# Decay rows of the second mixer: one pass over 64 stacked partitions in place of exact fp32 selection

## The chip, the cores and the metric

The kernel runs on one core of one Trainium2 chip. The time is device time in microseconds of one execution; lower is better. Engines are named as the profile names them: PE is TensorE, PEld its weight load, DVE is VectorE, ACT is ScalarE, POOL is GpSimd, SP is SyncE.

## The reference, cut to what matters

Two transformer-like blocks run one after the other on 512 tokens of width 1024. The change lies in the second block's mixer, in its state-space (Mamba-2) scan with 32 heads of width 64 in 4 groups of 8 heads. The kernel scans in chunks of 128 tokens, which computes the same thing as the reference's chunks of 64:

```python
da = (dt * a).reshape(b, L, G, J)
acs = jnp.cumsum(ak, axis=1)                       # per head, within a chunk
seg = acs[:, :, None] - acs[:, None, :]
decay = jnp.exp(jnp.where(causal, seg, -jnp.inf))
y_diag = jnp.einsum("blsg,blsgj,bsgjp->blgjp", cb, decay, xk)
y_off  = jnp.einsum("blgn,bgjpn,blgj->blgjp", ck, state, jnp.exp(acs))
```

Each head needs its row `acs` (512 values, one per token) on all 128 partitions (for `seg`), and each pair of heads needs its two rows on 64 partitions each (for `exp(acs)`).

## The kernel before, in words

Every engine has one hand-written instruction stream; semaphores order them. Where the same semaphore is reused under another name, the table `GOES_ON` says from which count. PE's stream sets the pace of the second mixer (`pe_mix2`): for each group g it runs the 14 projection units of group g+1 (a unit is 24 matmuls of 128x512: eight blocks of the contraction, each as upper by upper, lower by upper and upper by lower half) and weaves the scan of group g between them. For the last group the units are those of `gate_conv` and `conv_out` (`g_conv`, `conv_out` in the code).

A weight unit comes by DMA into one of six slots of `ring`; ACT copies its upper half into fp32r (`act_upper`), then POOL subtracts to get the lower half in place (`pool_lower`, the tensor `lo_ring`), and only then may PE start the unit (semaphore `split`).

For the scan of group g, with j from 0 to 3 for its pairs of heads and n = 4g + j:

- `all_acs(g, j)` on PE spreads the rows of the two heads of pair j to 128 partitions each: a matmul of `row_acs` (32 partitions, plain fp32) by a one-hot column of the identity, broadcast to 128 columns, and then on top of it an fp32r matmul (`ident_r` by `later_r`) that adds 2^60 above the diagonal.
- `off(g, j)` spreads the two rows of the pair to 64 partitions each (two fp32 matmuls into the two halves of one bank) and then multiplies the states (`y_off`, three fp32 matmuls).
- `diag(g, j)` is eight small fp32 matmuls; it waits for `seg` of DVE's `weighted(g, j)`.
- On ACT, `decays(g, j)` takes the exponentials (eight of 128x128 for `seg`, one of 128x512 for `exp_acs`). ACT reaches it after it has copied out the PE unit ahead of it (`z_out`, `raw_out`). After the exponentials comes the next `act_upper`.
- On DVE, `weighted`, `off_out` and `diag_out` consume what PE and ACT made. Between them DVE runs the 31 taps of the depthwise convolution of group g+1 (`taps`, reading PSUM banks 6 and 7), and after the last tap the 24 steps of the short convolution (`ssm_conv`, SBUF to SBUF). The next group's first unit writes into bank 6 and so waits for the last tap; the next group's taps wait for `gate_u`, that is for its units 1 and 3 and ACT's sigmoid.

PE's order in one group is: units 0 to 3; sums and transposes; units 4 to 6 with `new_state` and `turn_x`; `all_acs(g,0)`; unit 7; `off(g,0)`; `all_acs(g,1)`; and then four times a unit (8 to 11), `diag(g,j)`, `off(g,j+1)`, `all_acs(g,j+2)`; then units 12 and 13. A stretch from one of units 8 to 11 to the next is called a step below.

Of the kernel before, what the change touches and what calls it, by code (L numbers as in the profile page):

```python
# [17 lines left out]
P = 128  # L18
# [44 lines left out]
for _name, _n in COLUMNS:  # L63
# [6 lines left out]
    ("causal", 128), ("levels", 6 * 128), ("reset64", T), ("reset128", T),  # L70
    ("rank4", 4), ("rank8", 8), ("half_col", 2), ("slot_values", 16), ("rank_ids", 64),
]
# [8 lines left out]
for _name, _n in SMALLS:  # L81
# [159 lines left out]
    "expert_in": ("y_hi", 8),  # L241
    "sparse_silu": ("gates_hi", 1),
    "y_picked": ("gates_lo", 1),
}
# [16 lines left out]
def two_block_program(nc, x_d, w_d, mod_w_d, c_d, col_d, con_d, sma_d, lora_d, combine_d, h_d, y_d, x_kept_d, out_d):  # L261
    with ExitStack() as ctx:  # L262
# [24 lines left out]
        def halves(name, over, offset, *shape):  # L287


            return nc.alloc_sbuf_tensor_at(name, [P, *shape], F32R, offset=base[over] + 4 * offset)  # L290
# [1506 lines left out]
        later_r = halves("later", "con", CON["strict64"], P)  # L1797
        ident_r = halves("ident_r", "con", CON["eye64"], P)
        G_UNITS = 14
        X_ORDER = (4, 5, 0, 1, 2, 3)  # L1800
# [12 lines left out]
        def pe_mix2(pe, mm, flip, take, project, project_both, norm_add, rotation):  # L1813
# [47 lines left out]
            def all_acs(g, j):  # L1861
                for o in range(2):
                    h, m = SH * g + 2 * j + o, SH * g + 2 * j + o
                    out = take(("acs", m), ("seg_exp", m + 1))
                    mm(out[:, :], row_to_all(h, NE), row_acs[0:NE, :], True, False)
                    mm(out[:, :].rearrange("p (c t) -> p c t", c=TT), ident_r[:, :],
                       later_r[:, :].rearrange("p (a t) -> p a t", a=1).broadcast_to([P, TT, P]), False, True).then_inc(S("acs_done"), 1)

            def off(g, j):
                n = 4 * g + j  # L1870
                out = take(("exp_acs", n), ("exp_acs", n + 1))
                for o in range(2):
                    last = mm(out[64 * o:64 * o + 64, :], row_to_half(2 * n + o, NE), row_acs[0:NE, :])
                last.then_inc(S("pair_acs_done"), 1)
                out = take(("y_off", n), ("y_off", n + 1))
# [42 lines left out]
            for g in range(NG - 1):  # L1918
# [10 lines left out]
                if g == 0:  # L1929
                    pe.wait_ge(*at_count("ssm_cols", 2))  # L1930
                    pe.wait_ge(*at_count("later", 2))
                all_acs(g, 0)
# [78 lines left out]
        def act_mix2(act, steps):  # L2011
# [63 lines left out]
            def decays(g, j):  # L2075
# [13 lines left out]
                if n >= 2:  # L2089
                    act.wait_ge(*at_count("y_sum", n - 1))  # L2090
                act.activation(exp_acs[n % 2], bank[at[("exp_acs", n)]][:, :], ACT.Exp, scale=-1.0).then_inc(S("exp_acs"), 1)

            upper_through(first + 1)
# [10 lines left out]
            steps.wait()  # L2104
            act.activation(row_tmp[0:NE, :], row_tmp[0:NE, :], ACT.Ln, bias=column("one", rows=NE)).then_inc(S("dt_log"), 1)
            after("conv_a", 0, 0)
            act.wait_ge(*at_count("end_arg", 1))
# [114 lines left out]
        def dve_mix2(dve, steps, modulate, mod_bias):  # L2222
# [105 lines left out]
            def merge_conv(n):  # L2328
# [5 lines left out]
            dve.tensor_scalar(later_r[:, :], constant("causal"), -LATER, LATER, ALU.mult, ALU.add).then_inc(S("later"), 1)  # L2334
            dve.tensor_copy(ident_r[:, :], ident).then_inc(S("later"), 1)
            dve.wait_ge(*at_count("a_pos", 1))
            dve.wait_ge(*at_count("dt_log", 1))
# [12 lines left out]
                              ident[0:NE, 0:NE].rearrange("h (a c) -> h a c", c=1).broadcast_to([NE, NE, TT]),  # L2350
                              last_acs.rearrange("h (a c) -> h a c", a=1).broadcast_to([NE, NE, TT]), ALU.mult).then_inc(S("rows"), 1)
            dve.wait_ge(*at_count("end_exp", 1))
            dve.tensor_tensor(row_dtw[0:NE, :], row_tmp[0:NE, :], row_dt[0:NE, :], ALU.mult).then_inc(S("rows"), 1)
            gate_u(0)
            taps(0, 0, 16)
# [1008 lines left out]
```

## Time and profile before

| | |
|---|---|
| median of 3 runs | 1978.67 us (1976.53 to 1979.45) |
| time of the profiled execution | 1979.14 us |
| its span | 1977.5 us |
| granted clock of PE, mean over the span | 0.956 |
| PE busy | 1802.8 us (91%) |
| DVE busy | 972.1 us (49%) |
| ACT busy | 550.4 us (28%) |
| POOL busy | 851.1 us (43%) |

The time of an execution is 1.6 us more than its span. The mixer's scan lies between about 919 and 1358 us of the span; group 0 is scanned from 919, group 1 from 1032, group 2 from 1151, group 3 from 1270. A row of the trace of PE shows matmuls that overlap in its pipeline, so the distance between two starts, not the duration, is what a matmul takes of PE's time. One fp32 matmul of 512 columns shows as two records.

### The profile page before, as it was taken

The numbers are of one execution on the slowest core, as the hardware profiler recorded it, in microseconds if no ns is written. First come the engines' busy times: TensorE is split into PE (matmuls) and PEld (weight loads), VectorE is DVE, ScalarE is ACT, GpSimd is POOL, SyncE is SP. The second block draws the span as 40 slices with busy tenths as digits, with TensorE's granted clock in tenths as the row PEclk, the third lists the DMA queues.
The fourth block names the chain that finished last, engine by engine and source line by source line (L and its number), as shares of the span: only waits on it lengthen the run. The fifth ranks groups of instructions, "written<-read, shape, count | busy, mean of one in ns | idle before, by whom it ended". The sixth has DMA issues, their size and how long they took to land. (4 is left out here: it accounts for less than half of the span.)

```text
span 1977.5 us, 27738 instructions
## 1 busy us (share of the span) xinstructions
PE 1802.8 (91%) x10956; PEld 1283.4 (65%) x10956; DVE 972.1 (49%) x1363; ACT 550.4 (28%) x979; POOL 851.1 (43%) x408
## 2 busy tenths in 40 slices
PE   6999879998688785999999899999998999999997
PEld 4768668875233222677676676667776678888876
DVE  6476788452011112595767958554888331212101
ACT  3341452422222213423343423563100021010000
POOL 0421246240111110354242432423898668787874
PEclk8989899899799987999999999999999999999999
DMA  8821225315899997122121211213467223333331
GB/s 294 324 71 54 64 98 153 130 45 193 301 410 409 408 409 283 60 86 78 54 75 54 75 58 59 65 54 108 145 205 261 75 75 96 96 96 94 98 96 64
DMA packets 81758, 290.43 MB, mean 147 GB/s; under 512 B 11120, under 2 KB 11120, under 8 KB 81008
## 3 DMA queue, kind: packets, MB, share of 16 engines
q1 hardware_dynamic: 74880, 271.54, 39.5%
q10 hardware_dynamic: 2160, 8.91, 1.2%
q0 software_dynamic: 4608, 8.40, 1.1%
q8 instruction: 83, 1.36, 0.3%
q14 instruction: 27, 0.22, 0.0%
HBM read 282.25 MB, written 14.94 MB: 150 GB/s over the span
## 5 line engine op out<-in xcount | busy, mean ns | idle before, releaser
L2638 PE MATMUL bank<-arena 64*64 64x64 f32 (+4 forms) x1968 | 228.2, 377 | 53.1 <-ACT arena L1687 28.0
L2581 POOL TENSOR_TENSOR lo_ring<-ring,hi_ring 128x1024 fp32r<-128x1024 f32 x52 | 150.7, 2902 | 260.0 <-ACT hi_ring L2575 260.0
L2638 PE MATMUL bank<-h_lo,hi_ring 128*128 128x512 f32 x648 | 255.7, 395 | 0.0
L2638 PE MATMUL bank<-mix_h_hi,lo_ring 128*128 128x512 f32 x576 | 228.2, 396 | 0.0
L2638 PEld LDWEIGHTS bank<-arena 128*64 128x64 f32 (+2 forms) x1968 | 112.8, 156 | 157.1 <-issue 149.5
L2611 POOL TENSOR_TENSOR lo_ring<-ring,hi_ring 128x1024 fp32r<-128x1024 f32 x77 | 203.0, 2636 | 6.0
L2609 POOL TENSOR_TENSOR hi_ring<-ring,col 128x1024 fp32r<-128x1024 f32 x77 | 157.3, 2043 | 78.6 <-PE bank L2638 78.2
L2638 PE MATMUL bank<-mix_h_hi,hi_ring 128*128 128x512 f32 x416 | 166.8, 401 | 10.5 <-POOL lo_ring L2581 6.8
L2247 DVE SCALAR_TENSOR_TENSOR arena<-bank,col,arena 128x511 f32<-128x511 f32 (+14 forms) x240 | 156.5, 722 | 0.0
L2638 PEld LDWEIGHTS bank<-h_lo,hi_ring 128*128 128x128 f32 x648 | 122.2, 189 | 27.6
L2638 PE MATMUL bank<-ffn_h_hi,lo_ring 128*128 128x512 f32 x352 | 139.2, 395 | 0.0
L2638 PE MATMUL bank<-arena,con 64*64 64x64 f32 (+8 forms) x428 | 128.9, 476 | 3.6 <-DVE arena L1503 3.1
L2638 PEld LDWEIGHTS bank<-mix_h_hi,lo_ring 128*128 128x128 f32 x576 | 109.3, 190 | 25.1 <-issue 0.5
L1762 POOL DMA_INDIRECT y_dram<-arena,slot_table x16 | 16.1, 1004 | 222.6 <-DVE arena L1725 222.6
L2505 DVE TENSOR_TENSOR arena<-arena,bank 128x512 f32<-128x512 f32 x22 | 15.1, 687 | 189.7 <-PE bank L2638 189.7
L2581 POOL TENSOR_TENSOR lo_ring<-ring,hi_con 128x1024 fp32r<-128x1024 f32 x18 | 51.8, 2880 | 113.0 <-ACT hi_con L2575 113.0
L2638 PEld LDWEIGHTS bank<-mix_h_hi,hi_ring 128*128 128x128 f32 x416 | 78.5, 189 | 32.2 <-POOL lo_ring L2581 7.7
L2638 PE MATMUL bank<-ffn_h_hi,hi_ring 128*128 128x512 f32 x232 | 91.3, 394 | 0.0
L2642 PE MATMUL bank<-con,arena 128*128 128x128 f32 x320 | 52.3, 305 | 35.1 <-DMA arena<-h_dram,slot_table 14.9
L3084 DVE SCALAR_TENSOR_TENSOR arena<-arena,late 128x1024 f32<-128x1024 f32 x46 | 69.8, 1529 | 26.6 <-DMA arena<-mod_weights_dram 26.5
L2581 POOL TENSOR_TENSOR lo_ring<-ring,hi_ring_1a 128x1024 fp32r<-128x1024 f32 x10 | 26.7, 2674 | 126.4 <-ACT hi_ring_1a L2575 126.4
L1260 POOL TENSOR_TENSOR arena<-xT,con 128x256 f32<-128x256 f32 x48 | 52.1, 1108 | 66.4 <-DVE xT L1161 47.0
(435 smaller groups left out, 3777.6 us busy)
## 6 DMA issues: line engine op xcount, KB each, us to landing
ring<-weights_dram SPq DMA_DIRECT2D x248, 512.0 KB, 3.6
arena<-weights_dram SPq DMA_DIRECT2D x150, 512.0 KB, 11.3
arena<-mod_weights_dram SPq DMA_DIRECT2D x54, 512.0 KB, 4.7
late<-mod_weights_dram SPq DMA_DIRECT2D x42, 512.0 KB, 3.7
arena<-y_dram ACTq DMA_DIRECT2D x8, 512.0 KB, 6.8
xT<-x_dram SPq DMA_DIRECT2D x2, 1024.0 KB, 7.6
xT<-x_dram SPq DMA_DIRECT2D x1, 2048.0 KB, 9.8
h_dram<-arena ACTq DMA_DIRECT2D x4, 512.0 KB, 8.5
```

Of the source, the lines that this page charges most:

```text
L1260: pool.tensor_tensor(four(level_t[:, q, :]), four(ab[:, q, 0:256]), constant("levels", l, 64).rearrange("p (a t) -> p a t", a=1).broadcast ...
L1762: pool.indirect_dma_start(out=y_d, out_offset=bass.IndirectOffsetOnAxis(ap=slot_table[:, PAIRS + p:PAIRS + p + 1], axis=0), in_=y_rows[:, ...
L2247: dve.scalar_tensor_tensor(conv_y[:, k, back:T], u[:, 0:T - back], w, conv_y[:, k, back:T], ALU.mult, ALU.add).then_inc(S("conv_y"), 1)
L2505: dve.tensor_tensor(ffn_act[:, n, :], ffn_silu[:, n % 2, :], bank[at[("ffn_up", n)]][:, :], ALU.mult).then_inc(S("ffn_act"), 1)
L2581: pool.tensor_tensor(ring_r[:, u % RING, :], ring[:, u % RING, :], hi_unit(u).bitcast(F32), ALU.subtract).then_inc(S("split"), 1)
L2609: pool.tensor_tensor(hi, w, column("zero").broadcast_to([P, UNIT]), ALU.add).then_inc(S("split_hi"), 1)
L2611: pool.tensor_tensor(ring_r[:, u % RING, :], w, hi.bitcast(F32), ALU.subtract).then_inc(S("split"), 1)
L2638: return pe.matmul(out, lhsT, rhs, start=start, stop=stop, skip_group_check=True)
L2642: return pe.matmul(out, x, ident, start=True, stop=True, is_transpose=True, skip_group_check=True)
L3084: dve.scalar_tensor_tensor(w, w, 1.0, silu_c2 if 48 <= i < MOD_OUT else silu_c, ALU.mult, ALU.mult, accum_out=mod[:, mod_column(i):mod_col ...
```

## The change

`all_acs` and `off` no longer use plain fp32. The row `acs` is split into an upper part in fp32r (partitions 0 to 31 of `acs_r`) and the rest (partitions 32 to 63), and the selector has two ones per column (`head_r`: the identity of 32 stacked twice), so that one fp32r matmul over 64 partitions adds both parts. For a pair of heads the selector is a 64x128 tile `two_heads_r`, two of them in turn; ACT writes each (64x128) from `head_r`, two pairs ahead. So the pair needs one matmul in place of two. `acs_r` overlays the constant `reset128`, `head_r` the constant `rank_ids` (which is moved for that), the selectors overlay `head_ones` and a part of `sma`. DVE gets three instructions, once: `head_r`, and the upper and lower part of `acs_r`. ACT gets 16.

```diff
-    ("rank4", 4), ("rank8", 8), ("half_col", 2), ("slot_values", 16), ("rank_ids", 64),
+    ("rank_ids", 64), ("rank4", 4), ("rank8", 8), ("half_col", 2), ("slot_values", 16),
...
+        acs_r = halves("acs_r", "con", CON["reset128"], T)
+        head_r = halves("head_r", "con", CON["rank_ids"], NE)
+        two_heads_r = [halves("two_heads0", "con", CON["head_ones"], P), halves("two_heads1", "sma", T, P)]
...
                     out = take(("acs", m), ("seg_exp", m + 1))
-                    mm(out[:, :], row_to_all(h, NE), row_acs[0:NE, :], True, False)
+                    mm(out[:, :], head_r[0:2 * NE, h:h + 1].broadcast_to([2 * NE, P]), acs_r[0:2 * NE, :], True, False)
...
                 out = take(("exp_acs", n), ("exp_acs", n + 1))
-                for o in range(2):
-                    last = mm(out[64 * o:64 * o + 64, :], row_to_half(2 * n + o, NE), row_acs[0:NE, :])
-                last.then_inc(S("pair_acs_done"), 1)
+                pe.wait_ge(*at_count("two_heads", n + 1))
+                mm(out[:, :], two_heads_r[n % 2][0:2 * NE, :], acs_r[0:2 * NE, :]).then_inc(S("pair_acs_done"), 1)
...
-                    pe.wait_ge(*at_count("later", 2))
+                    pe.wait_ge(*at_count("later", 5))
...
                 act.activation(exp_acs[n % 2], bank[at[("exp_acs", n)]][:, :], ACT.Exp, scale=-1.0).then_inc(S("exp_acs"), 1)
+                if n + 2 < 4 * NG:
+                    two_heads(n + 2)
+
+            def two_heads(n):
+
+                act.activation(two_heads_r[n % 2][0:2 * NE, :].rearrange("p (o a) -> p o a", o=2),
+                               head_r[0:2 * NE, 2 * n:2 * n + 2].bitcast(F32).rearrange("p (o a) -> p o a", a=1).broadcast_to([2 * NE, 2, 64]),
+                               ACT.Copy).then_inc(S("two_heads"), 1)
...
+            act.wait_ge(*at_count("later", 3))
+            two_heads(0)
+            two_heads(1)
             after("conv_a", 0, 0)
...
+            dve.tensor_tensor(head_r[0:2 * NE, :], ident[0:2 * NE, 0:NE], ident[0:2 * NE, NE:2 * NE], ALU.add).then_inc(S("later"), 1)
...
+            dve.tensor_copy(acs_r[0:NE, :], row_acs[0:NE, :]).then_inc(S("later"), 1)
             dve.wait_ge(*at_count("end_exp", 1))
             dve.tensor_tensor(row_dtw[0:NE, :], row_tmp[0:NE, :], row_dt[0:NE, :], ALU.mult).then_inc(S("rows"), 1)
+            dve.wait_ge(*at_count("later", 4))
+            dve.tensor_tensor(acs_r[NE:2 * NE, :], row_acs[0:NE, :], acs_r[0:NE, :].bitcast(F32), ALU.subtract).then_inc(S("later"), 1)
             gate_u(0)
```

On PE, between unit 7 and unit 8 of a group, these rows stand before the change (`arena,con` is `row_acs` by the one-hot column; the row of three is `y_off`):

```order
L2638 MATMUL bank<-arena,con 64x512 x2
L2638 MATMUL bank<-arena 128x128 x3
L2638 MATMUL bank<-arena,con 128x512
L2638 MATMUL bank<-later,ident_r 128x512
L2638 MATMUL bank<-arena,con 128x512
L2638 MATMUL bank<-later,ident_r 128x512
L2638 MATMUL bank<-mix_h_hi,hi_ring_51 128x512
```

And with the change at the same place (all line numbers below the new lines are 18 higher):

```order
L2656 MATMUL bank<-acs_r,two_heads_84 128x512
L2656 MATMUL bank<-arena 128x128 x3
L2656 MATMUL bank<-acs_r,head_r 128x512
L2656 MATMUL bank<-later,ident_r 128x512
L2656 MATMUL bank<-acs_r,head_r 128x512
L2656 MATMUL bank<-later,ident_r 128x512
L2656 MATMUL bank<-mix_h_hi,hi_ring_51 128x512
```

Nothing changed its place; two half matmuls became one, and each selecting matmul reads `acs_r` in fp32r.

On ACT, in the first `decays` of group 0, these rows stand with the change; the row L2100 is the new selector, and behind it comes the upper half of the next weight unit (L2593):

```order
L2037 ACTIVATE arena<-bank 128x512
L2088 ACT_TABLE_LOAD
L2088 ACTIVATE arena<-bank,arena 128x128 x8
L2094 ACTIVATE rstd<-bank 128x512
L2100 ACTIVATE two_heads_84<-head_r 64x128
L2593 ACTIVATE hi_ring_51<-ring 128x1024
```

Before, L2575 (the same `act_upper`) followed directly on L2091 (the exponential of `exp_acs`); everything else on ACT kept its order.

## Rows read from the trace of the kernel before

**Rows 1.** The page, part 1: engine, busy us, share, instructions.

```profile
PE 1802.8 (91%) x10956; PEld 1283.4 (65%) x10956; DVE 972.1 (49%) x1363; ACT 550.4 (28%) x979; POOL 851.1 (43%) x408
```

**Rows 2.** Waits of PE in the scan, 900 to 1360 us: us, times, longest.

```profile
PE bank L2638 <- POOL lo_ring L2581: 10.4, 2, 5.7
...
PE bank L2638 <- DVE arena L2247: 1.4, 1, 1.4
```

**Rows 3.** Timeline of PE, three unit starts: start us, us, work, [idle, releaser].

```profile
1120.52 0.47 PE L2638 MATMUL bank<-mix_h_hi,hi_ring 128*128 128x512 f32 x1 [1.40 <-DVE arena L2247]
...
1137.57 0.79 PE L2638 MATMUL bank<-mix_h_hi,hi_con 128*128 128x512 f32 x1 [5.72 <-POOL lo_ring L2581]
...
1259.38 0.79 PE L2638 MATMUL bank<-mix_h_hi,hi_ring 128*128 128x512 f32 x1
```

**Rows 4.** Timeline of POOL, and one row of ACT's.

```profile
1079.70 2.69 POOL L2581 TENSOR_TENSOR lo_ring<-ring,hi_ring 128x1024 fp32r<-128x1024 f32 x1 [5.37 <-ACT hi_ring L2575]
...
1127.56 9.96 POOL L2581 TENSOR_TENSOR lo_ring<-ring,hi_con 128x1024 fp32r<-128x1024 f32 x1 [9.92 <-ACT hi_con L2575]
...
1248.65 12.30 POOL L2581 TENSOR_TENSOR lo_ring<-ring,hi_ring 128x1024 fp32r<-128x1024 f32 x2 [6.44 <-ACT hi_ring L2575]
...
1067.06 2.17 ACT L2085 ACTIVATE arena<-bank,arena 128x128 f32<-128x128 f32 x8
```

**Rows 5.** Timeline of DVE, from group 1's first weighted on.

```profile
1068.30 0.69 DVE L2302 TENSOR_TENSOR arena<-arena 128x512 f32<-128x512 f32 x1 [6.87 <-ACT arena L2085]
...
1077.26 0.69 DVE L2302 TENSOR_TENSOR arena<-arena 128x512 f32<-128x512 f32 x1 [1.69 <-ACT arena L2085]
1078.22 0.69 DVE L2302 TENSOR_TENSOR arena<-arena 128x512 f32<-128x512 f32 x1 [0.27 <-ACT arena L2085]
...
1080.20 2.74 DVE L2320 TENSOR_TENSOR arena<-arena,late 128x512 f32<-128x512 f32 x1
...
1100.10 0.69 DVE L2302 TENSOR_TENSOR arena<-arena 128x512 f32<-128x512 f32 x1 [1.43 <-ACT arena L2085]
...
1114.62 6.38 DVE L2247 SCALAR_TENSOR_TENSOR arena<-bank,col,arena 128x486 f32<-128x486 f32 x10
...
1131.25 4.05 DVE L2263 SCALAR_TENSOR_TENSOR arena<-arena,col 128x512 f32<-128x512 f32 x6
```

**Rows 6.** Waits of DVE in the scan, 900 to 1360 us.

```profile
DVE arena L2302 <- ACT arena L2085: 43.2, 24, 9.6
```

**Rows 7.** Groups by form, PE, 936 to 1345 us: records, busy us, mean ns.

```profile
L2638 PE MATMUL bank<-arena,con 32*128 32x512 f32 x64 | 35.8, 639 | 0.0
...
L2638 PE MATMUL bank<-arena,con 32*64 32x512 f32 x64 | 17.2, 612 | 0.0
```

**Rows 8.** Timeline of PE, group 1, unit 7 to unit 8: start us, us.

```profile
1065.04 1.07 PE L2638 MATMUL bank<-arena,con 32*64 32x512 f32 x4
1066.04 0.94 PE L2638 MATMUL bank<-late,arena 128*128 128x128 f32 x6
1066.91 1.12 PE L2638 MATMUL bank<-arena,con 32*128 32x512 f32 x2
1067.96 0.50 PE L2638 MATMUL bank<-later,ident_r 128*128 128x512 f32 x1
1068.39 1.12 PE L2638 MATMUL bank<-arena,con 32*128 32x512 f32 x2
1069.44 0.50 PE L2638 MATMUL bank<-later,ident_r 128*128 128x512 f32 x1
1069.78 0.40 PE L2638 MATMUL bank<-mix_h_hi,hi_ring 128*128 128x512 f32 x1
1070.02 0.39 PE L2638 MATMUL bank<-mix_h_hi,lo_ring 128*128 128x512 f32 x1
```

**Rows 9.** Stages: us, busy of engines, granted clock.

```profile
1137.50:1142.00 4.50, 4.43 (x13) 3.60 (x14) 0.69 (x1) 1.41 (x2) 4.50 (x3) 0.66 0.00 0
1142.00:1146.00 4.00, 4.00 (x19) 3.20 (x19) 0.00 (x0) 1.06 (x1) 0.21 (x1) 1.00 0.01 1
```

More of the change, by code:

```diff
@@ L242 @@
     "sparse_silu": ("gates_hi", 1),
+    "two_heads": ("totals", 1),
     "y_picked": ("gates_lo", 1),
```

## The prediction

> **What bounds the kernel now.** The page's busy times come first: PE is busy for 1802.8 us of 1977.5, every other engine (PE's own weight load aside) for less than half [rows 1]. So time taken from PE should be time won, unless PE is waiting where the change works. The waits of PE in the scan are few, 10.4 us for POOL's `lo_ring` in two waits and 1.4 us for DVE's taps (L2247) in one [rows 2], but the timeline shows where they stand, and that matters more than their sum. Behind group 1 PE waits 1.40 us at 1120.52, before unit 0 of the next group, for the last taps, and 5.72 us at 1137.57, before unit 2, for POOL [rows 3]. The other wait for POOL, of 4.7 us, is the same one behind group 0.
>
> Why is POOL late? Its subtraction of one weight tile takes 2.69 us at 1079.70, but 9.96 us at 1127.56 and 12.30 us for two at 1248.65 [rows 4]. In both stretches DVE runs its convolution from SBUF to SBUF without a pause, until 1131.25 + 4.05 = 1135.3 in the first [rows 5], and POOL ends at 1127.56 + 9.96 = 1137.5, 2.2 us after DVE stopped. The two exclude each other. It holds the other way too: DVE's L2320 takes 2.74 us at 1080.20 while POOL subtracts from 1079.70 to 1082.4, against 0.69 for another product of the same shape (L2302) [rows 4, 5]. That names the mechanism: the next group's unit 2 is released by DVE's last convolution step, with POOL between them. The Trainium skill says the same (GPSIMD Engine Reference, Specifications): GpSimd's SBUF interfaces are shared with VectorE, and the contention is with DVE instructions that have two SBUF inputs or run in a two-port mode; by that rule the taps, which read PSUM, leave POOL alone, and the trace agrees.
>
> So from `gate_u` of one group to unit 2 of the next the pace is DVE's: taps, the scan's products, taps, convolution, POOL's 2.2 us. PE has a margin of 5.72 us there, DVE has only its waits. Those are on `weighted` (L2302), which waits for ACT, which waits for PE's unit to end: 43.2 us in 24 waits over the four groups [rows 6]. In group 1 they are 6.87 us at 1068.30, 1.69 at 1077.26, 0.27 at 1078.22 and 1.43 at 1100.10 [rows 5].
>
> **The change on PE.** It removes 64 records of 32\*128 (two per matmul, so 32 matmuls) and 64 of 32\*64 [rows 7], and puts in 32 + 16 matmuls in fp32r. The sequence of one `all_acs` runs from 1066.91 to 1069.78, 2.87 us: exact 1.05, masking 0.43, exact 1.05, masking 0.34 [rows 8]. The trace has no fp32r matmul over 64 partitions. Nearest are the projections, 1069.78 to 1070.02, 0.23 to 0.24 us with weight load hidden [rows 8], and the masking matmul, 0.34 behind an exact one and before an fp32r one, 0.43 between two exact ones. From below 4 x 0.23 = 0.92, from above 4 x 0.43 = 1.72. I take 0.34 + 3 x 0.23 = 1.03, since only the first follows an fp32 matmul: 1.84 us won, 16 times. `off` pays 1.00 us for its selection (1065.04 to 1066.04); one fp32r matmul costs 0.43 behind `diag` (three of four) and, because the unit before it hands over faster, about 0.22 behind unit 7: 3 x 0.57 + 0.78 = 2.5 us per group. Together 4 x 1.84 + 2.5 = 9.9 us per group, 39.5 us over four. If instead the new matmul cost nothing less than an exact one, PE would win only the second half of `off` or nothing; that is the other end.
>
> A rule of the Trainium skill prices the same in another way (FP8 and Floating Point Precision, TensorE Precision Notes): a true fp32 matmul makes four passes through the array, one of reduced precision takes one. By it 48 matmuls save three passes each, an estimate of 48 x 3 x 0.23 = 33 us; the rows give more, since 1.05 us is over four times 0.23.
>
> **What of it arrives.** In groups 0 to 2 the next units wait for DVE's chain, so only what DVE waits less counts. `weighted(g,0)` is released by unit 7, which comes 1.84 us earlier (one `all_acs`): the wait falls from 6.87 to 5.0. Each of the following steps is shorter on PE by 1.84 + 0.78 or 0.57, 2.4 to 2.6 us, more than the waits of 1.69 and 1.43 there, which vanish, and with them three gaps of 0.27 between the two heads, as ACT is then ahead. Sum: 1.84 + 1.69 + 1.43 + 3 x 0.27 = 5.8 us per group. From then on DVE has no idle time between the first `weighted` and the end of its convolution, and the remaining 4 us of PE's gain turn into longer waits at `diag`, at unit 0 of the next group (1.40 us in group 1, then some 4) and before unit 2.
>
> Group 0: 5.8. Group 1: 5.8. In group 2 the fp32 sums of the layer norm stand ahead of the unit in question (`g_conv` 2, at 1259.38 [rows 3]); the two subtractions at 1248.65 take 12.30 us, the second of them undisturbed and so about 2.69, and the first, which this unit needs, is done at 1248.65 + 12.30 - 2.69 = 1258.3 [rows 4]. PE was later than POOL by 1.1. With the change POOL is ready at 1252.5 and PE at 1259.4 - 9.9 = 1249.5: 6.9 us won, and a new wait of 3.0. Group 3 has no taps beside it and its convolution is over; there PE sets the pace and all 9.9 arrive. The sum is 5.8 + 5.8 + 6.9 + 9.9 = 28.4 us.
>
> **What is added elsewhere.** ACT gets 16 copies of 64x128. Eight exponentials of 128x128 take 2.17 us, 0.27 each [rows 4], so a copy costs about 0.3. It stands behind `exp_acs`, where ACT then waits for PE's unit anyway; what it delays is `act_upper`, and POOL's subtraction by 0.3, whose tile PE needs only two units later. DVE's three instructions come once, before `gate_u(0)`; no larger than the 128x512 ones of 0.69 [rows 5], and `gate_u` behind them waits for ACT's sigmoid. I cost both at nothing; without that cover they would be 0.3 on each of nine steps, 2.7 us, and at most 3 x 0.69 = 2.1 once.
>
> **Collisions.** POOL's subtraction now starts earlier within a step while DVE runs a little later relative to it, so it no longer meets `diag_out` but may meet `weighted`. Each meeting costs 2.74 - 0.69 = 2.05 us [rows 5]. Three of them per group are in the trace already. I keep three; one less or one more in each of three groups is 6 us either way. The clock: after the wait of 5.72 us PE is granted 0.66 of full speed over the next 4.5 us, so it ran at 1.2 GHz for a part, and then 1.00 [rows 9]; that costs (1 - 0.66) x 4.5 = 1.5 us, and the new wait of 3.0 us in group 2 may bring one more such dip.
>
> Against the profiled execution: 1979.14 - 28.4 = 1950.7. The median of the runs shown is 0.5 us below that execution, less than the runs differ among themselves. I say 1951.
>
> **The rivals.**
> (a) *Forecast*: DVE's chain holds back three groups; 1951, own range 1946 to 1957. Chance 0.55.
> (b) *PE's whole gain arrives*: if the waits for POOL and the taps shrink as much as PE's work, 39.5 us are won: 1939.6. For it speaks PE's 91% busy; against it that PE already waits at 1120.52 and 1137.57, where earlier arrival only lengthens the wait. Partly true if collisions vanish. Chance 0.10, with values from 1939 to 1946.
> (c) *New collisions and dips eat a third*: one more meeting in each of three groups (6 us), a dip in group 2 and another (3 us), loads not hidden in group 3 (4 x 0.7 = 3 us): 28 - 12 = 16 won, 1963; values from 1957 to 1970. For it: a saturated DVE has no idle time left to absorb a meeting. Chance 0.28.
> (d) *No change*: the fp32r matmul over 64 partitions with a broadcast selector costs what it replaces, 32 x 1.05 + 16 x 1.00 = 49.6 us over 48 matmuls, or 1.03 each. Against it: the masking matmul has a broadcast operand too and costs 0.43 at most [rows 8]. 1979; chance 0.03.
> (e) *Slower*: it costs more than those 1.03 us, because the stationary operand, 64 partitions read with a stride of zero, loads slowly in fp32r and nothing hides it. From 1.03 on every further tenth costs 48 x 0.1 = 4.8 us, all of it on PE, which then sets the pace everywhere; at 1.2 us the time is 1979 + 8 = 1987. For it: no row shows such a load. Against it: the one-hot column of before is read the same way, and its load is inside the 1.05. Chance 0.04.
>
> **How the numbers follow.** A difference of 0.2% (4 us) is about what a measurement of this kernel can tell from none. Range: (a) whole, the upper part of (b), the lower half of (c): 1943 to 1961, about 0.79 of the chance. Faster: 0.55 + 0.10 + 0.28 = 0.93; within: 0.03; slower: 0.04.
>
> **What the profile of the changed kernel would show.** Right: the 32 selecting matmuls at 0.23 to 0.43 us from start to start and a step on PE 2.4 us shorter where PE does not wait; no wait of DVE for ACT at L2302 other than the first of a group (near 5 us); in groups 0 to 2 waits of PE at unit 0 of the next group for taps and before unit 2 for POOL, larger in sum than the 10.4 + 1.4 us of now; group 3 shorter by 9.9. Wrong: waits on PE in groups 0 to 2 no longer than now (then (b)); more than three products of DVE over 2 us per group, or a granted clock under 1 in new places (then (c)); a selecting matmul near 1 us (then (d)). The forecast fails above all if DVE's chain is not as full as I read it.

## The result and the profile after

The changed kernel takes 1963.86 us in the median of 6 runs (1960.05 to 1965.68), the kernel before 1980.6 in 6 (1976.53 to 1987.8): a ratio of 0.9923, 95% interval 0.9903 to 0.9942, so about 15 us faster where 28 were forecast. The profiled execution took 1965.68 us with a span of 1964.0, 13.5 less than before.

The page of the changed kernel, part 1, as [rows 1]:

```profile
PE 1783.6 (91%) x10876; PEld 1287.4 (66%) x10876; DVE 990.5 (50%) x1366; ACT 553.5 (28%) x995; POOL 845.9 (43%) x408
```

PE is busy 19.2 us less, not 39.5. Between unit 7 and unit 8 a new wait now breaks the sequence of [rows 8]; one step later, between unit 8 and unit 9 of group 1, it runs through, behind `diag` in place of a unit (start us, us):

```profile
1067.83 0.49 PE L2656 MATMUL bank<-acs_r,two_heads 64*128 64x512 f32 x1
1068.25 0.94 PE L2656 MATMUL bank<-late,arena 128*128 128x128 f32 x6
1069.11 0.49 PE L2656 MATMUL bank<-acs_r,head_r 64*128 64x512 f32 x1
1069.53 0.50 PE L2656 MATMUL bank<-later,ident_r 128*128 128x512 f32 x1
1069.96 0.50 PE L2656 MATMUL bank<-acs_r,head_r 64*128 64x512 f32 x1
1070.39 0.50 PE L2656 MATMUL bank<-later,ident_r 128*128 128x512 f32 x1
1070.73 0.39 PE L2656 MATMUL bank<-mix_h_hi,hi_ring 128*128 128x512 f32 x1
```

From 1069.11 to 1070.73 `all_acs` takes 1.62 us; before it was 2.87, and 1.03 was forecast. Each selecting matmul takes 0.42 or 0.43, and so does the masking one between them. The start of `off` takes 0.42 instead of 1.00, as forecast; behind unit 7 it is 0.42 too (1056.73 to 1057.15), where 0.22 was forecast.

The timeline of PE at its waits around group 1, as [rows 3]:

```profile
1010.09 0.80 PE L2656 MATMUL bank<-mix_h_hi,hi_ring 128*128 128x512 f32 x1 [5.69 <-POOL lo_ring L2599]
...
1059.94 0.49 PE L2656 MATMUL bank<-acs_r,head_r 64*128 64x512 f32 x1 [1.01 <-ACT arena L2088]
...
1111.73 0.76 PE L2656 MATMUL bank<-mix_h_hi,hi_ring 128*128 128x512 f32 x1 [5.46 <-DVE arena L2261]
...
1128.78 0.79 PE L2656 MATMUL bank<-mix_h_hi,hi_con 128*128 128x512 f32 x1 [3.02 <-POOL lo_ring L2599]
```

The wait at 1111.73 was 1.40 us, and the one of 1.01 is new: the second `all_acs` of a group wants a bank that ACT's exponentials have yet to read. It comes at 947.00 and 1179.00 too, with 1.00.

The timeline of DVE in group 1, as [rows 5]; L2316 is `weighted`, L2334 and L2332 are in `diag_out`, L2340 is `group_out`:

```profile
1059.99 0.69 DVE L2316 TENSOR_TENSOR arena<-arena 128x512 f32<-128x512 f32 x1 [5.62 <-ACT arena L2088]
...
1068.64 0.69 DVE L2316 TENSOR_TENSOR arena<-arena 128x512 f32<-128x512 f32 x1 [1.37 <-ACT arena L2088]
...
1071.59 2.77 DVE L2334 TENSOR_TENSOR arena<-arena,late 128x512 f32<-128x512 f32 x1
...
1081.85 1.99 DVE L2332 TENSOR_TENSOR late<-late,rstd 128x384 f32<-128x384 f32 x1
...
1090.74 2.50 DVE L2332 TENSOR_TENSOR late<-late,rstd 128x384 f32<-128x384 f32 x1
...
1094.35 4.88 DVE L2340 SCALAR_TENSOR_TENSOR arena<-arena,col 128x512 f32<-128x512 f32 x4
```

The first wait is 5.62, not 5.0, and the second 1.37, not nothing. An undisturbed L2332 takes 0.56 and four of L2340 2.73 (both in the run with late evacuations below), so these four meetings with POOL cost 2.08 + 1.43 + 1.94 + 2.15 = 7.6 us, and with one more of 0.91 at 1103.72 it is 8.5, where before there were three, 6.2 us.

**An account of PE.** The three stretches below run from `gate_u` of one group to `gate_u` of the next, and the last to the first matmul of `ssm_out`. First the kernel before, then the changed one (stretch, us, PE busy, records, granted clock, DMA share, GB/s):

```profile
918.14:1031.49 113.35, 108.66 (x494) 0.98 0.22 65
1031.49:1150.98 119.49, 112.37 (x507) 0.99 0.20 62
1150.98:1385.69 234.71, 234.06 (x1037) 1.00 0.23 72
```

```profile
914.93:1024.43 109.50, 102.61 (x474) 0.97 0.22 68
1024.43:1143.49 119.06, 109.37 (x487) 0.94 0.21 62
1143.49:1367.64 224.15, 221.63 (x996) 0.99 0.24 75
```

Time minus busy is PE's idle time. One minus the clock, times the stretch, is what the lower clock cost; busy minus that is the work, as at full clock. Over the whole scan, with the clock read in 46 equal slices of each trace (its rounding is then worth a few tenths, where these three rows give 12.7 for the changed kernel's loss):

| kernel | scan | work | clock loss | idle |
|---|---|---|---|---|
| before | 467.6 | 451.6 | 3.5 | 12.5 |
| changed | 452.7 | 421.8 | 11.8 | 19.1 |

So 29.8 us of work are gone, 8.3 came back as clock and 6.6 as idle: 14.9. Outside the scan the changed execution came to it 3.2 us earlier in code that nothing touched, and took 596.4 us behind it where before it was 591.8; the other runs here have 592 to 597 there, so I read nothing into either. A single profile is coarse: ahead of the scan, in code that nothing touched, the clock loss alone lies between 68 and 87 us over the 17 profiles. In slices of 1 us, every stretch of lowered clock in the scans of fourteen of these traces costs 1.7 us or two or three times that; the kernel before pays 1.7 us twice, the changed one seven times. Over whole executions, with the clock and the span of each, seven of the changed kernel (the first run of the next section) lose 100.4 us on average and the 21 of the kernel before beside them 95.9: some 5 us more, rather than 8.3.

### The profile page after: what moved, and what is told of

It is laid out like the page before. It is cut to its first block and busy times, and to the rows that moved or that the text cites. A ratio compares the mean times of both kernels' runs of the same rounds, so it can differ in the third digit from the quotient of the medians.

```text
span 1964.0 us, 27613 instructions
## 1 busy us (share of the span) xinstructions
PE 1783.6 (91%) x10876; PEld 1287.4 (66%) x10876; DVE 990.5 (50%) x1366; ACT 553.5 (28%) x995; POOL 845.9 (43%) x408
## 3 DMA queue, kind: packets, MB, share of 16 engines
q10 hardware_dynamic: 2160, 8.91, 1.2%
## 5 line engine op out<-in xcount | busy, mean ns | idle before, releaser
L2599 POOL TENSOR_TENSOR lo_ring<-ring,hi_ring 128x1024 fp32r<-128x1024 f32 x52 | 145.4, 2799 | 247.3 <-ACT hi_ring L2593 247.3
L2629 POOL TENSOR_TENSOR lo_ring<-ring,hi_ring 128x1024 fp32r<-128x1024 f32 x77 | 203.4, 2641 | 6.0
L2656 PE MATMUL bank<-mix_h_hi,hi_ring 128*128 128x512 f32 x416 | 168.1, 404 | 14.8 <-POOL lo_ring L2599 5.8
L3102 DVE SCALAR_TENSOR_TENSOR arena<-arena,late 128x1024 f32<-128x1024 f32 x46 | 77.7, 1701 | 21.6 <-DMA arena<-mod_weights_dram 21.4
L1726 DVE COPY arena<-bank 128x512 f32<-128x512 f32 x32 | 22.1, 692 | 115.3 <-PE bank L2656 115.3
## 6 DMA issues: line engine op xcount, KB each, us to landing
xT<-x_dram SPq DMA_DIRECT2D x1, 2048.0 KB, 10.3
```

The source lines that it names most:

```text
L1726: dve.tensor_copy(y_rows[:, par, half * 512:half * 512 + 512], bank[4 + half][:, :]).then_inc(S("sparse_y"), 1)
L2599: pool.tensor_tensor(ring_r[:, u % RING, :], ring[:, u % RING, :], hi_unit(u).bitcast(F32), ALU.subtract).then_inc(S("split"), 1)
L2629: pool.tensor_tensor(ring_r[:, u % RING, :], w, hi.bitcast(F32), ALU.subtract).then_inc(S("split"), 1)
L2656: return pe.matmul(out, lhsT, rhs, start=start, stop=stop, skip_group_check=True)
L3102: dve.scalar_tensor_tensor(w, w, 1.0, silu_c2 if 48 <= i < MOD_OUT else silu_c, ALU.mult, ALU.mult, accum_out=mod[:, mod_column(i):mod_col ...
```

## The experiments

The table gives all runs; a ratio is to the kernel before on the same chip beside them (1983.6 us for the first four rows; 1981.2 for dummy matmuls to 19 taps; 1981.65 for off alone and the three combined kernels; 1981.37 for the last three). The four columns at the right are the account, each from its own profiled execution. The four groups of runs come from four chips, so kernels of different groups are best compared by their ratios.

| run | median us | ratio (95%) | scan | work | clock loss | idle |
|---|---|---|---|---|---|---|
| changed, again | 1964.8 | 0.9916 (0.9886 to 0.9947) | 449.6 | 421.7 | 8.5 | 19.4 |
| 128 rows | 1957.33 | 0.9866 (0.9819 to 0.9913) | 444.1 | 407.9 | 10.1 | 26.1 |
| late evacuations | 1971.15 | 0.9931 (0.9911 to 0.9952) | 461.9 | 419.1 | 15.4 | 27.5 |
| all_acs alone | 1968.71 | 0.9928 (0.9905 to 0.9951) | 452.1 | 432.0 | 5.1 | 15.0 |
| dummy matmuls | 1963.17 | 0.9912 (0.9887 to 0.9938) | 449.3 | 431.1 | 6.7 | 11.4 |
| early exponentials | 1955.92 | 0.9885 (0.9857 to 0.9913) | 443.9 | 422.4 | 5.1 | 16.5 |
| before, 19 taps | 1972.88 | 0.9946 (0.9915 to 0.9977) | 462.2 | 451.0 | 5.1 | 6.0 |
| changed, 19 taps | 1954.11 | 0.9854 (0.9815 to 0.9894) | 445.1 | 421.7 | 6.9 | 16.5 |
| off alone | 1984.3 | 1.0016 (0.9992 to 1.0041) | 473.9 | 440.4 | 17.3 | 16.2 |
| 128 rows + early | 1945.26 | 0.9835 (0.9800 to 0.9871) | 431.6 | 406.0 | 6.8 | 18.8 |
| ... + late evacuations in two groups | 1941.83 | 0.9813 (0.9778 to 0.9847) | 430.8 | 404.9 | 8.5 | 17.4 |
| 128 rows + early + dummy matmuls | 1940.07 | 0.9811 (0.9774 to 0.9847) | 428.7 | 414.9 | 3.4 | 10.4 |
| off + early | 1979.6 | 0.9989 (0.9964 to 1.0014) | 465.1 | 440.2 | 10.1 | 14.7 |
| before + early | 1979.9 | 0.9977 (0.9954 to 1.0000) | 467.6 | 450.0 | 5.2 | 12.4 |
| off alone, again | 1986.55 | 1.0018 (0.9994 to 1.0042) | 472.2 | 441.5 | 13.8 | 16.9 |

The column of work is the steadiest: kernels with the same matmuls agree within 3.3 us (419.1 to 422.4 for the changed one and its variants), so smaller differences in it mean nothing.

**The changed kernel again.**

> The changed kernel once more, unaltered, so that the other kernels of this call have it beside them on the same chip. Every theory expects the same time as before within its scatter: 1960 to 1966 us, 0.990 to 0.995 of the kernel before.

1964.8 us, as expected. Its scan is 3.1 us shorter than in the first profile with the same work and idle: the clock alone differed (8.5 against 11.8). That is the grain of a single profile.

**Selectors over 128 partitions.** `acs_r` and `head_r` get zeros in rows 64 to 127, and the two matmuls read all rows:

```diff
-                    mm(out[:, :], head_r[0:2 * NE, h:h + 1].broadcast_to([2 * NE, P]), acs_r[0:2 * NE, :], True, False)
+                    mm(out[:, :], head_r[:, h:h + 1].broadcast_to([P, P]), acs_r[:, :], True, False)
...
-                mm(out[:, :], two_heads_r[n % 2][0:2 * NE, :], acs_r[0:2 * NE, :]).then_inc(S("pair_acs_done"), 1)
+                mm(out[:, :], two_heads_r[n % 2][:, :], acs_r[:, :]).then_inc(S("pair_acs_done"), 1)
```

> The selectors, acs_r and head_r now take all 128 partitions (rows 64 to 127 are zero), nothing else moves. Theory A (a weight load of 64 partitions between matmuls of 128 is not hidden behind the matmul before it): the selecting matmul of two_heads and that of head_r show 0.23 to 0.30 us from the end of the one before to their own, where the changed kernel shows 0.42 to 0.43; a mixer unit's PE work falls by about 0.4 us for all_acs and 0.15 to 0.2 per off start. Rival B (the gap comes from the type or from the stride-zero selector): it stays 0.42. On the time both expect little, as DVE's chain ends the group: A 1958 to 1964 us, B 1960 to 1966.

The timelines tell it best. First PE's and its weight load's rows of the run with 128 rows, in `all_acs` ahead of unit 7:

```profile
1050.60 0.48 PE L2657 MATMUL bank<-acs_r,head_r 128*128 128x512 f32 x1
1050.91 0.40 PE L2657 MATMUL bank<-later,ident_r 128*128 128x512 f32 x1
1051.14 0.40 PE L2657 MATMUL bank<-acs_r,head_r 128*128 128x512 f32 x1
1051.38 0.40 PE L2657 MATMUL bank<-later,ident_r 128*128 128x512 f32 x1
1051.61 0.39 PE L2657 MATMUL bank<-mix_h_hi,hi_con 128*128 128x512 f32 x1
...
1050.91 0.19 PEld L2657 LDWEIGHTS bank<-acs_r,head_r 128*128 128x128 f32 x1
1051.15 0.19 PEld L2657 LDWEIGHTS bank<-later,ident_r 128*128 128x128 f32 x1
```

Then the weight loads of the changed kernel, whose matmuls stand further up:

```profile
1069.53 0.19 PEld L2656 LDWEIGHTS bank<-later,ident_r 128*128 128x128 f32 x1 [0.24 <-issue]
1069.96 0.18 PEld L2656 LDWEIGHTS bank<-acs_r,head_r 64*128 64x128 f32 x1 [0.25 <-issue]
```

With 64 rows each load begins only with its own matmul's row (1069.53, 1069.96) and adds its 0.18 to 0.19 us; with 128 rows it begins one matmul ahead (1050.91 for the matmul of 1051.14) and is hidden, and matmuls follow each other at 0.23 or 0.24, only the first taking 0.31. The type, the broadcast selector and the number of columns are the same in both. The steps at 1050.91 and 1051.38 show 0.23 for the masking matmul too, which the change did not touch: it pays 0.43 between two neighbours of another height, and 0.34 with one behind it only (1070.39 to 1070.73). The pair's selector takes 0.23 behind unit 7 and 0.33 or 0.34 behind the small matmuls of `diag`. Theory A holds and rival B is out; both operands got their 128 rows together, so which of the two counts is not separated. With 1.01 us the whole `all_acs` (1050.60 to 1051.61) now costs what was forecast. The work falls by another 14 us and the time by 7.5, to just below the range of theory A; the rest is idle time again, and the waits for ACT at the second `all_acs` grow from 1.00 to 1.78 us, because PE now comes earlier. DVE's first `weighted` waits 4.82 and 4.85 us here, near the 5.0 of the forecast.

**Evacuations held back.** ACT's `raw_out` of rows 1 to 3, behind which stands `act_upper`, waits for DVE's `off_out` (row 3 in groups 2 and 3 of the units for `group_out`):

```diff
             def raw_out(g, r):
                 i = X_ORDER[r]
+                if g and 0 < r < 4:
+                    act.wait_ge(*(at_count("y_ssm", 4 * (g - 1)) if r == 3 and g > 1 else at_count("y_off", 4 * (g - 1) + r + 1)))
```

> ACT's evacuation in raw_out of rows 1 to 3 is held until DVE has finished its off_out (row 3 in groups 2 and 3: its group_out), so that POOL's subtraction starts later and no longer lies in DVE's weighted and off work. Theory C (meetings of POOL and DVE took the gain back: L2334 2.77 us, L2332 1.99 and 2.50, group_out 4.88 us in group 1 of the changed kernel): DVE's chain from gate_u to the taps' end gets up to 5 us shorter per group, and the time falls by 5 to 15 us, to 1948 to 1958 us. Rival D (meetings only move: POOL's subtraction meets the taps and then holds PE, as PE's 9.96 us wait for POOL in the kernel before): no gain or a loss, 1962 to 1975 us, with longer PE waits for POOL.

Both theories have a part. Rows of this kernel's timelines (DVE in group 1's `diag_out` and `group_out`; then PE, behind group 2):

```profile
1088.87 0.56 DVE L2334 TENSOR_TENSOR late<-late,rstd 128x384 f32<-128x384 f32 x1
...
1090.54 2.73 DVE L2342 SCALAR_TENSOR_TENSOR arena<-arena,col 128x512 f32<-128x512 f32 x4
...
1237.88 0.80 PE L2658 MATMUL bank<-mix_h_hi,hi_ring 128*128 128x512 f32 x1 [11.37 <-POOL lo_ring L2601]
```

In group 1 the meetings are down to 1.3 us from the 8.5 of the changed kernel, but the chain from `gate_u` to the next `gate_u` is 101.6 us against 104.8: of 7.2 us freed, 3.2 arrive and 3.6 became longer waits of DVE (19.2 us against 15.6). But behind group 2 POOL now subtracts inside DVE's convolution, and PE waits 11.37 us with the clock falling behind it. The meetings are real, but taking them away is worth only 1 to 3 us a group; moving POOL's work costs more where it then meets the convolution.

**The two halves apart.** One kernel keeps `head_r` in `all_acs` and puts the two plain fp32 matmuls back into `off`; the other keeps `two_heads` in `off` and puts `row_acs` back into `all_acs`:

```diff
-                mm(out[:, :], two_heads_r[n % 2][0:2 * NE, :], acs_r[0:2 * NE, :]).then_inc(S("pair_acs_done"), 1)
+                for o in range(2):
+                    last = mm(out[64 * o:64 * o + 64, :], row_to_half(2 * n + o, NE), row_acs[0:NE, :])
+                last.then_inc(S("pair_acs_done"), 1)
```

> Only half of the change undone otherwise: head_r for the off starts stays, all_acs goes back to two fp32 matmuls of 64 columns on row_acs per pair of heads, and ACT's copies of two_heads are gone. Theory (the gain comes on DVE's first weighted wait and on PE in proportion to what all_acs saved, 1.25 us of it per unit, off starts the rest): weighted waits 6.85 us again, PE's sum 16 x 1.25 = 20 us longer than in the changed kernel, and the time 1970 to 1976 us. Rival E (ACT's copies cost what they save, or the gain is from off alone): 1960 to 1966 us, like the changed kernel.

My text describes this kernel the wrong way round. What ran has the new `all_acs` and the old `off`, as the diff shows and as its name says; the ACT copies are gone, as written. Its numbers are to be read so: 1968.71 us, of 19.6 us of work saved 15.5 arrive in the scan. On top of it the new `off` brings 3.9 us by the medians (1964.8 with both), but the intervals of the two ratios overlap. In group 1 it even costs: without it `group_out` meets no subtraction, the meetings are 5.8 us and not 8.5, and DVE's chain is 102.4 us and not 104.8.

> The other half of the change: off's start by two_heads stays, with ACT's copies; all_acs takes row_acs in two fp32 selecting matmuls as in the kernel before. By the account of PE from the runs so far (the scan gets shorter by the work saved, less what PE's waits over 0.3 us grow, less half of the time at clock 0.50 that is added), with 16 x 0.57 = 9.1 us saved and waits like the kernel before: 7 to 9 us of the scan, 1970 to 1976 us. Rival (the gain came from the half with all_acs and the ACT copies cost time of their own): no gain, 1978 to 1982 us.

The half in `off` brings nothing: 1984.3 us beside 1981.65, and again:

> Off's start alone once more, unaltered, to see whether its result (1984.3 us) and its clock dips come again: by theory J both do, 1980 to 1986 us with half clock for 20 us or more of the scan; if it was one bad hour of the chip, 1970 to 1976 us.

It repeats, 1986.55 us. Of the work 11.2 and 10.1 us are saved, but 13.8 and 10.3 more than before are lost to the clock and 3.7 and 4.4 to idle. All executions say the same: by their own clocks the ten of each run lose 10.8 and 10.3 us more than the kernel before beside them, and the rest of their time is 7.3 and 6.9 us shorter. The windows of PE in the first of the two runs (stretch, us, PE busy, records, granted clock), around group 1's and group 2's second `all_acs`, where PE waits 0.38 and 0.37 us for ACT:

```profile
1064.00:1068.00 4.00, 3.62 (x13) 0.98 0.46 133
1068.00:1072.00 4.00, 4.00 (x9) 0.50 0.00 0
1072.00:1076.00 4.00, 4.00 (x13) 0.66 0.01 4
...
1192.00:1196.00 4.00, 3.63 (x7) 0.77 0.31 122
1196.00:1200.00 4.00, 4.00 (x10) 0.50 0.00 0
```

So PE ran at 1.2 GHz for a part of it. In the kernel before the same slices around its own place (1060 to 1072) are at 1.00; it has still more of the plain fp32 matmuls, but no wait for ACT there. All six such waits of 0.37 or 0.38 us in the two profiles have a dip beside them. In the run with the new `all_acs` alone PE waits 0.42 us for ACT at the same three places and none has one, so a wait of that length does not do it by itself. Not all of the loss is the clock's, either. In group 1 DVE's chain sets the pace, and it is 111.8 and 110.3 us here against 106.5: its meetings with POOL are 9.7 us instead of 6.2, with `group_out` among them:

```profile
1107.12 4.87 DVE L2340 SCALAR_TENSOR_TENSOR arena<-arena,col 128x512 f32<-128x512 f32 x4
```

The dip suggested theory J, and two more kernels:

> The kernel with off's start alone changed (1984.3 us, no gain, with PE's clock at 0.50 to 0.80 behind each second all_acs, where PE waits 0.37 us for ACT), plus ACT's early exponentials, which take that wait away. Theory J (the small wait for ACT amid the sparse matmuls of the unit is what pulls the clock, and the clock is what ate the 9.1 us that off saves): the stretches 951 to 957, 1068 to 1076 and 1192 to 1204 stay at 1.00, and it is 8 to 14 us faster than the kernel before with the same ACT order. Rival K (the clock falls there for the narrow matmuls themselves, or the saving goes to DVE's chain and POOL): the dips stay, or the two kernels are within 3 us.

> The kernel before with ACT's early exponentials alone, the partner of the run above. Its PE already had no wait for ACT and no dip there, so by theory J the new order brings it only what DVE's chain gets shorter: 2 to 6 us, 1974 to 1979 us. If DVE's chain alone decided, as my first account had it, it would gain 12 to 15 us, 1965 to 1969 us.

Their order of ACT is that of the next experiment. With the wait gone there is no dip at the two later places, but one is left at the first, where PE waits for nothing, and there is another from 1295 to 1299. The windows of the run with off and early exponentials:

```profile
955.00:960.00 5.00, 5.00 (x14) 0.73 0.01 2
...
1186.00:1192.00 6.00, 6.00 (x37) 1.00 0.30 87
```

Between the two, 9.8 us of work are saved, 4.9 go to the clock and 2.3 to idle, and the scan is 2.6 us shorter; the medians, 1979.6 and 1979.9 us, do not tell them apart, which is what rival K said. Over their ten executions each the one with `off` loses 5.5 us more to the clock, about half of the 10.3 to 10.8 without the early exponentials, so theory J is at most half of it. That the clock takes back much of `off`'s saving is in all three traces; what pulls it down I have not settled. The new meetings of group 1 are there too (8.9 us against 5.4), so that up to the last stretch nothing arrives even with the wait gone (113.5 and 119.8 us against 113.4 and 119.5).

**Exponentials earlier on ACT.** In groups 0 to 2:

```diff
-                for i in range(4):
+                for i in range(3):
                     z_out(g + 1, i)
                 if g:
                     act.preload_act_table_set(LN_EXP)
+                upper_through(at[("unit", "z", g + 1, 3)] + 1)
                 decays(g, 0)
+                z_out(g + 1, 3)
                 if g:
+                    act.preload_act_table_set(LN_EXP)
                     gain_out(g - 1)
...
+                seg_exps(g, 1)
                 raw_out(g + 1, 0)
-                for j in range(1, 4):
+                row_exp(g, 1)
+                raw_out(g + 1, 1)
+                for j in range(2, 4):
```

> The changed kernel, with ACT's order alone altered in groups 0 to 2: the eight exponentials of heads 0 and 1 and exp_acs stand ahead of the last z evacuation, and the exponentials of heads 2 and 3 ahead of the first raw_out; it costs ACT one more table load of 1.28 us each way. Theory H (what binds a group is DVE's chain, whose biggest remaining waits are those for ACT's exponentials, 5.6 and 1.4 us, and PE's new wait of 1.0 us for ACT at the second all_acs): the first weighted no longer waits for the exponentials, off_out waits about 1.5 us in its place, the second weighted waits nothing, PE's 1.0 us at 947.00, 1059.94 and 1179.00 is gone, DVE's chain is 4 to 5 us shorter per group, and the time falls by 12 to 15 us, to 1949 to 1953 us. Rival I (POOL and its meetings with DVE, or PE, bind instead): under 5 us of gain, 1959 to 1965 us.

1955.92 us, 8.9 less than the changed kernel on another chip, 6 by the ratios (0.9885 and 0.9916), and short of the 12 to 15. Its waits on DVE (timeline, group 1; L2337 is `off_out`):

```profile
1052.65 1.28 DVE L2330 TENSOR_TENSOR arena<-arena 128x512 f32<-128x512 f32 x2
1056.56 0.55 DVE L2337 TENSOR_TENSOR rstd<-rstd,bank 128x384 f32<-128x384 f32 x1 [2.62 <-PE bank L2670]
...
1075.07 0.69 DVE L2330 TENSOR_TENSOR arena<-arena 128x512 f32<-128x512 f32 x1 [2.00 <-ACT arena L2092]
```

The wait of 5.62 became 2.62 for PE, and a new one of 2.00 came two steps on. The waits of PE for ACT are gone, the idle time is 2.9 us less than in the run again, the clock loss 3.4. With the plain fp32 forms the same order brings nothing in the scan (467.6 us, as before): there DVE waits 4.46 us for PE at `off_out` and 4.44 for ACT at the third `weighted`. That ACT's order matters only once PE's steps are short is what these two profiles suggest; the whole times (0.9977, up to 1.0000) leave room for a gain of some us with the old forms too.

**Dummy matmuls ahead of PE's waits.**

```diff
+                    if key in WARM:
+                        out = take(key, freed_by, b)
+                        for _ in range(WARM[key]):
+                            mm(out[:, :], mix_h_hi_r[:, 0, 0:P], mix_h_hi_r[:, 1, :])
                     pe.wait_ge(*at_count("split", unit[0] - unsplit[0]))
```

> The changed kernel, with dummy matmuls of 512 columns ahead of PE's two waits for POOL (22 of them at 1010.09, whose wait is 5.69 us, and 12 at 1128.78, 3.02 us), into the bank that the unit behind them overwrites. Theory F (the long waits of PE cost a second time, by the granted clock of 0.50 behind them: 6.8 us at half clock each, where the kernel before had 3.4 us): the two stretches behind stay at 1.00, gate_u's wait for its second gate goes from 13.2 and 13.6 back to 12.3 us, and the time falls by 2 to 3 us beside the changed kernel, to 1961 to 1963 us. Rival G (DVE's chain is late anyway, or the dip comes whatever PE does): within 1 us of the changed kernel, 1963.5 to 1965.5 us.

The mechanism shows: `gate_u`'s second waits are 10.93 and 10.97 us, as with no dip. The price does not: 1963.17 us (ratio 0.9912) cannot be told from the 1964.8 (0.9916) without them, since the dip behind the 5.45 us wait for the taps stays and the run again had lost only 8.5.

**Nineteen taps.** The convolution's loop ends after 19 of 31 taps, which leaves 12 out:

```diff
-                for back in range(lo, hi):
+                for back in range(min(lo, NT), min(hi, NT)):
```

> The kernel before with 19 instead of 31 taps in the second mixer's convolution (12 taps of both channel blocks are left out of each group, so its output is another), which takes about 15 us off DVE's chain per group. With the next kernel it tells what PE's saving is worth where DVE does not bind: PE's waits at 1018, 1120 and 1137 (4.69, 1.40, 5.72 us) should shrink, to 1960 to 1970 us.

> The changed kernel with the same 19 taps. Theory H again (PE's saving, 16 x (1.25 + 0.57) = 29 us less 3 us of new waits for ACT, is real and was hidden behind DVE's chain): 24 to 28 us faster than the kernel before with 19 taps. Rival (the saving is lost to PE's clock and to waits for POOL, not to DVE's chain): the same 14 to 19 us between the two as with 31 taps.

The kernel before gains less than expected, and the two differ by 18.8 us, 17.1 in the scan: the size that the rival gave. The scans are the firmer evidence; the whole times scatter too much (1959.6 to 1982.2 in ten runs, 1945.4 to 1962.1 in four) to exclude the 24 to 28 of theory H. The work saved is again 29.3. In the first stretch, where PE waits for POOL 0.52 and 0.53 us, 109.36 us became 102.00, and 7.4 is the whole saving of four pairs (4 x 1.83); in the last, the wait for POOL before unit 2 grew from 3.98 to 8.91 us. Without DVE's taps POOL behind DVE's convolution is the next bound.

**Together.**

> The 128-row selectors of one run and the early exponentials of another together. If the two terms are independent (7.5 and 8.9 us in their runs): 1946 to 1950 us. Rival (both free the same wait, so that they do not add up): 1953 to 1956 us.

1945.26 us, a little below the range: the two add up (1964.8 - 7.5 - 8.9 is 1948.4; by the ratios, 0.9866 + 0.9885 - 0.9916 is 0.9835, as measured).

> The kernel with 128 rows and early exponentials, and ACT's evacuations of rows 1 to 3 held for DVE's off_out in groups 0 and 1 alone (not in group 2, where the hold made PE wait 11.37 us for POOL). Theory C (meetings cost DVE 5 to 10 us per group): 2 to 5 us faster than without the hold. Rival D (POOL's later work holds PE at the third unit of the next group instead): the same or up to 5 us slower.

> The kernel with 128 rows and early exponentials, and dummy matmuls (20 and 14) ahead of PE's waits for POOL at the third unit of groups 2 and 3. Theory F (each long wait costs again by the clock behind it): the waits there fall under 1.5 us, gate_u's second wait to 10.9 us, 1 to 3 us faster than without them. Rival G: no change of over 1 us.

1941.83 and 1940.07 us; against 1945.26 the medians say 3 and 5 us, but the runs of the three overlap (1939.9 to 1945.2 and 1938.8 to 1946.1 against 1941.8 to 1950.5). The windows of the last kernel show the clock held behind both waits for POOL, where the changed kernel has 0.50 in 1010 to 1013 and 1128.7 to 1132:

```profile
1002.30:1005.30 3.00, 2.96 (x13) 1.00 0.00 0
1113.50:1117.00 3.50, 3.45 (x15) 1.00 0.00 0
```

At 0.981 of the kernel before, the last has the lowest median found here.

## Why the prediction was off, point by point

The sign, the mechanism of the POOL and DVE chain, and the longer waits for the taps and for POOL (14.4 us in place of 11.8 in groups 0 to 2) were right; the size was not: 15 us came where 28.4 were forecast, which is my rival (c), near its 1963. By the account, in the scan: 28.4 forecast, less 9.7 of work, less 8.3 of clock, plus 4.5 of idle that grew less than I had it (6.6 instead of 11.1), is 14.9. That account says what PE's time went to, not what held each stretch. By the forecast's own stretches it reads as follows; the middle column is the same sum with 1.25 us for an `all_acs` and 0.58 for an `off`, as measured:

| stretch | forecast | with measured matmuls | came |
|---|---|---|---|
| group 0 | 5.8 | 5.2 | 3.9 |
| group 1 | 5.8 | 5.2 | 0.4 |
| group 2, up to `g_conv` 2 | 6.9 | 6.3 | 3.9 |
| from there on | 9.9 | 7.3 | 6.6 |
| sum | 28.4 | 24.0 | 14.8 |

So the mis-sized matmuls take 4.4 of the 13.6 us that are missing. The single largest miss is group 1, 4.8 us: DVE's chain there got 1.7 shorter and not 5.2, and 1.3 were lost on top before the second `gate_u`, whose units ran behind a wait in a dip of the clock.

- **"I take 0.34 + 3 x 0.23 = 1.03"** is the term that failed first. It is 1.62, so 1.25 us are saved and not 1.84: 16 x 0.59 = 9.4 us of PE's work, and 4 x 0.2 = 0.8 more for the four `off` behind unit 7. The price I thought special to an fp32 neighbour is that of a neighbour over another number of partitions; the run with 128 rows shows it, and there, with the 1.01 us that I had forecast, the time is 7.5 us lower and inside my range. The upper bound, 1.72, was the right end. The 0.57 for `off` behind `diag` held (0.58).
- **"The wait falls from 6.87 to 5.0"**: 5.60 to 5.62, the same error at its next station; 4.82 to 4.85 with 128 rows.
- **"The waits of 1.69 and 1.43 vanish, with three gaps of 0.27"**: half wrong. The one of 1.69 stayed at 1.37, because PE, now early, waits 1.0 us for the bank that ACT's exponentials hold. I had looked only at who waits for PE, not at what PE would be too early for. The 1.43 did vanish, and two of the four gaps of 0.27 in group 1.
- **"I keep three meetings"**: right in group 0 (5.4 us against 6.2 before), wrong in group 1 (8.5 against 6.2, and 8.5 in the run again), where `group_out` was added. So from `gate_u` to `gate_u` the chain got 4.8 us shorter in group 0 and 1.7 in group 1, each time against 5.8. With the evacuations held back it got another 1 to 3 us shorter.
- **The clock** was costed at nothing in the sum and 3 us in a rival. It took 8.3 us (5.0 in the run again, and about 5 over whole executions). Behind the 5.72 us of before the clock was 0.66 over 4.5 us [rows 9], behind the waits of 5.46 and 3.02 us after each other it was 0.50 and then 0.57 to 0.67 (1111.7 to 1118 and 1128.7 to 1136). The loss does not follow the length of the wait: behind 5.72 us it was 1.7, behind 3.02 us 3.4, and in the run again behind 3.27 us nothing (1.00 from 1131.7 to 1139). So the wait that a saving turns into can cost a second time.
- **Group 3, "all 9.9 arrive", and group 2, "6.9 us won, and a new wait of 3.0"**: the last stretch, both together, is 10.6 us shorter and not 16.8; of 8 x 1.83 = 14.6 us by the measured sizes, 2.2 went to the clock and 1.9 to idle. The new wait of 3.0 did not come: counted from the second `gate_u` behind group 1, POOL was ready 3.2 us earlier than before and not 5.8, PE started the unit 3.9 earlier, and it waited 0.16.
- **ACT's copies** at nothing: not disproved. The run with the new `all_acs` and without them is 3.9 us slower, not faster, though it has the old `off` too.
- The account of the taps as the bound was too simple. With 12 of them out, PE's gain in the scan is 17.1 us, between the 14.9 and 18.0 of the two profiles with all taps, so no rise shows; POOL behind the convolution is next in line.

What stays open is why the clock falls amid the sparse matmuls of `off` alone, and why the same wait in the same kernel is followed by a dip in one execution and by none in another.

## What to carry to other kernels

Price a matmul by neighbours that have its number of partitions as well as its type, and if the stationary operand is short, try zero rows up to the height of its neighbours: here that was worth 7.5 us with nothing else moved. When a saving ends in a wait, write down three prices for it: the wait, the clock behind the wait, and what the early engine now finds not ready; and make the account of work, clock loss and idle for both kernels, since it told at once which of them had eaten the gain.

## What the hardware showed unexpectedly

A weight load between two matmuls of different height (64 against 128 partitions) was not hidden: 0.42 to 0.43 us a matmul, against 0.23 with equal heights. And 10 us less work on PE, in narrow exact matmuls, did not make one kernel faster in either of its two measurements, 20 executions (ratios 1.0016 and 1.0018), with 10 to 14 us more lost to the clock in the scan, which stood at 0.50 in places that had 1.00 before.
